# Two narrow columns as the held operand of a norm sum, and weight slices used for both halves in turn

## The reference

```python
def rms_norm(x, gain):
    xf = x.astype(jnp.float32)
    xf = xf * lax.rsqrt(jnp.mean(xf * xf, axis=-1, keepdims=True) + RMS_EPS)
    return (xf * gain.astype(jnp.float32)).astype(x.dtype)
...
        h = h + hierarchical_moe(rms_norm(h, norm_ffn_g[layer]), ...)
    return rms_norm(h, norm_final_g)
...
        h = rmsnorm(x, attn_norm[l])
        q, k, v, g, gk_low, s5_u, rg_x, rg_gate = jnp.split(h @ w_in[l], splits, axis=-1)
...
def conv_ffn(h, w_up, conv_w, conv_b, w_down):
    up, gv = jnp.split(h @ w_up, 2, axis=-1)
    up = causal_dwconv(up, conv_w, conv_b)
    return (jax.nn.gelu(up) * gv) @ w_down
```

## Time and profile before

| | |
|---|---|
| median of 3 runs | 2604.46 us (2601.79 to 2614.28) |
| profiled execution | 2602.0 us |
| its span, first to last instruction | 2600.2 us |
| mean granted TensorE clock | 0.959 |
| TensorE busy | 2436.9 us (94%), 10998 matmuls, 10998 weight loads |
| VectorE busy | 1039.6 us (40%) |
| ScalarE busy | 571.8 us (22%) |
| GpSimd busy | 700.2 us (27%) |

### The profile page before, as it was taken

The page is one execution under the profiler, slowest core; times in us unless marked ns, Lnnn a source line. Parts: engine busy times, 40 slices in busy tenths (PEclk is TensorE's granted clock), DMA queues, the critical chain, the costliest instruction groups (busy, mean ns, idle before and its releaser), DMA issues.

```text
span 2600.2 us, 27514 instructions
## 1 busy us (share of the span) xinstructions
PE 2436.9 (94%) x10998; PEld 1768.3 (68%) x10998; DVE 1039.6 (40%) x1771; ACT 571.8 (22%) x760; POOL 700.2 (27%) x456
## 2 busy tenths in 40 slices
PE   5999999999798599999799999899899999999997
PEld 4888799999675244444644337644588888888885
DVE  6894044445443011111476866621422122122124
ACT  3001265666522111110121004100211011011011
POOL 2332434346120200000302862001133332332321
PEclk9999999999899799999599999789899999999998
DMA  3132122223304566821501110001111111111101
GB/s 139 66 118 94 42 68 72 72 83 110 134 33 162 228 270 270 316 96 73 190 31 49 74 49 30 12 17 37 44 49 37 61 49 37 61 49 37 61 25 73
DMA packets 74348, 228.68 MB, mean 88 GB/s; under 512 B 5168, under 2 KB 36912, under 8 KB 69232
## 3 DMA queue, kind: packets, MB, share of 16 engines
q1 hardware_dynamic: 55712, 141.19, 15.6%
q0 software_dynamic: 12896, 61.09, 6.6%
q10 hardware_dynamic: 5616, 24.64, 2.3%
HBM read 173.42 MB, written 53.48 MB: 87 GB/s over the span
## 4 chain that ended last, share of the span: by engine, by line
PE 91%; DVE 4%; issue 2%; DMA 1%; ACT 1%; POOL 0%; SPq 0%; DVEq 0%; POOLq 0%
PE ps L657 13%; PE ps L659 13%; PE ps L658 13%; PE ps L619 11%; PE ps L814 8%; PE ps L741 7%; PE ps L830 4%; PE ps L723 4%; PE ps L732 3%; PE ps L667 2%; PE ps L639 2%; PE ps L900 1%; PE ps L919 1%; PE ps L805 1%; PE ps L851 1%
## 5 line engine op out<-in xcount | busy, mean ns | idle before, releaser
L657 PE MATMUL ps<-work_part 128*128 128x512 f32 x1472 | 574.3, 390 | 8.9 <-POOL work_part L503 7.2
L659 PE MATMUL ps<-work_part 128*128 128x512 f32 x1472 | 573.3, 389 | 0.0
L658 PE MATMUL ps<-work_part 128*128 128x512 f32 x1120 | 436.4, 390 | 0.0
L501 POOL CAST work_part<-ring 128x1024 fp32r<-128x1024 f32 (+2 forms) x108 | 105.9, 981 | 1055.2 <-PE ps L659 642.4
L657 PEld LDWEIGHTS ps<-work_part 128*128 128x128 f32 x1472 | 276.6, 188 | 67.8 <-issue 8.4
L659 PEld LDWEIGHTS ps<-work_part 128*128 128x128 f32 x1472 | 276.7, 188 | 57.5
L619 PE MATMUL ps<-work,ring 128*128 128x512 f32 x640 | 278.2, 595 | 1.4 <-DVE work L1935 1.4
L503 POOL TENSOR_TENSOR work_part<-ring,work_part 128x1024 fp32r<-128x1024 f32 (+2 forms) x108 | 241.9, 2239 | 8.6
L658 PEld LDWEIGHTS ps<-work_part 128*128 128x128 f32 x1120 | 210.6, 188 | 43.8
L619 PEld LDWEIGHTS ps<-work,ring 128*128 128x128 f32 x640 | 122.1, 191 | 154.8 <-issue 152.9
L814 PE MATMUL ps<-work 128*128 x496 | 219.2, 595 | 1.2 <-SPq L454 0.9
(11 more groups left out here) (309 smaller groups left out, 3023.8 us busy)
## 6 DMA issues: line engine op xcount, KB each, us to landing
work<-w_moe SPq DMA_DIRECT2D x16, 3072.0 KB, 11.0
ring<-w_up_units SPq DMA_DIRECT2D x44, 512.0 KB, 3.3
ring<-w_in_units SPq DMA_DIRECT2D x42, 512.0 KB, 3.3
x_slots<-hT SPq DMA_DIRECT2D x31, 512.0 KB, 3.5
work<-x_slots POOLq DMA_DIRECT2D x31, 512.0 KB, 4.6
y_slots<-work ACTq DMA_DIRECT2D x31, 512.0 KB, 2.6
ring<-w_down_units SPq DMA_DIRECT2D x24, 384.0 KB, 3.0
s_turns<-work ACTq DMA_DIRECT2D x8, 1024.0 KB, 4.0
```

What stands on the lines that cost most here:

```text
L501: pool.tensor_copy(WHI[n % 2][:, 0:cols], w).then_inc(whi_ready, 1)
L657: pe.matmul(ps[:, c], whi[:, w], hi[k][:, c], start=(k == 0), stop=False)
L658: pe.matmul(ps[:, c], whi[:, w], lo[k][:, c], start=False, stop=False)
L659: mm = pe.matmul(ps[:, c], wlo[:, w], hi[k][:, c], start=False, stop=(k == len(hi) - 1))
```

## The change

In the norm sums the operands trade places: the two columns `gain_sums[:, :, k]` are the held weights, the squares stream. The result has the tokens along a row, 2 x 128; ScalarE copies it into `TROW` (two partitions of a free work tile). Behind the last sum eight small transposes (use `P_TTURN`, one wait for each copy) turn it back into 128 x 2 for each tile, and VectorE reads these from PSUM. In `parts_tile` the loop over k is outside; each of the three products is made for both halves before the next, so a weight slice is named by consecutive matmuls: four with `whi`, two with `wlo`. The wait for `ready` stays once for each k.

```diff
--- before.py
+++ after.py
@@ -276,6 +276,7 @@
                 P_YSUM[tt] = take(1)
             if tt >= 1:
                 P_TSUM[tt - 1] = take(1)
+        P_TTURN = take(1)
         P_BOTH, P_FIRST = take(1), take(1)
 
         MAIN = [take(1) for _ in range(3)]
@@ -336,6 +337,7 @@
             emptied[use_s[u]], emptied[use_t[u]], emptied[use_o[u]] = (scores_ready, u + 1), (pT_ready, u + 1), (heads_done, u + 1)
         for i in range(NT):
             emptied[use_f[i]] = (f_ready, i + 1)
+        emptied[P_TTURN] = (tvar_ready, 1)
         emptied[P_BOTH], emptied[P_FIRST] = (hn_ready, NT), (hres_ready, NT)
         emptied[P_LOGIT] = (logit_ready, 1)
         emptied[P_ROUTE], emptied[P_RANK] = (gdiff_ready, 1), (rank_read, 1)
@@ -426,6 +428,7 @@
         YG = [Wp[13 + i] for i in range(2 * NT)]
         TSQ = [Wp[2], Wp[3]]
         TDIAG = [Wp[23], Wp[24]]
+        TROW = Wp[4][0:2, :]
         gain_sums = small[:, 0:2, :]
         both_gains = small[:, 2, :]
         tsums = small[:, 4:6, :]
@@ -648,14 +651,16 @@
                 ps, s = slot(n), split_of[u]
                 pe.wait_ge(wlo_ready, s + 1)
                 whi, wlo = WHI[s % 2], WLO[s % 2]
-                for half in range(2):
-                    c = slice(half * HALF, (half + 1) * HALF)
-                    for k in range(len(hi)):
-                        if ready is not None and half == 0:
-                            pe.wait_ge(ready, base + k + 1)
-                        w = slice(k * P, (k + 1) * P)
+                halves = [slice(half * HALF, (half + 1) * HALF) for half in range(2)]
+                for k in range(len(hi)):
+                    if ready is not None:
+                        pe.wait_ge(ready, base + k + 1)
+                    w = slice(k * P, (k + 1) * P)
+                    for c in halves:
                         pe.matmul(ps[:, c], whi[:, w], hi[k][:, c], start=(k == 0), stop=False)
+                    for c in halves:
                         pe.matmul(ps[:, c], whi[:, w], lo[k][:, c], start=False, stop=False)
+                    for c in halves:
                         mm = pe.matmul(ps[:, c], wlo[:, w], hi[k][:, c], start=False, stop=(k == len(hi) - 1))
                 mm.then_inc(mm_done, 1)
 
@@ -848,9 +853,14 @@
                     pe.wait_ge(tsq_ready, t)
                     ps = slot(P_TSUM[t - 1])
                     for k in range(NT):
-                        mm = pe.matmul(ps[:, 0:2], TSQ[(t - 1) % 2][:, k * P:(k + 1) * P], gain_sums[:, :, k],
+                        mm = pe.matmul(ps[0:2, 0:P], gain_sums[:, :, k], TSQ[(t - 1) % 2][:, k * P:(k + 1) * P],
                                        start=(k == 0), stop=(k == NT - 1))
                     mm.then_inc(mm_done, 1)
+            ps = slot(P_TTURN)
+            for t in range(NT):
+                pe.wait_ge(tsum_taken, t + 1)
+                mm = pe.transpose(ps[:, 2 * t:2 * t + 2], TROW[:, t * P:(t + 1) * P], ident[0:2, 0:2])
+            mm.then_inc(mm_done, 1)
             for i, n in enumerate((P_BOTH, P_FIRST)):
                 pe.wait_ge(tdiag_ready, i + 1)
                 ps = slot(n)
@@ -1183,7 +1193,7 @@
                                    ACT.Square).then_inc(tsq_ready, 1)
                 if t >= 1:
                     act.wait_ge(mm_done, done(P_TSUM[t - 1]))
-                    act.activation(tsums[:, :, t - 1], PS[P_TSUM[t - 1] % SLOTS][:, 0:2], ACT.Copy).then_inc(tsum_taken, 1)
+                    act.activation(TROW[:, (t - 1) * P:t * P], PS[P_TSUM[t - 1] % SLOTS][0:2, 0:P], ACT.Copy).then_inc(tsum_taken, 1)
             act.wait_ge(tvar_ready, 1)
             act.activation(troots, tsums, ACT.Sqrt).then_inc(troot_ready, 1)
             act.wait_ge(hn_ready, NT)
@@ -1738,9 +1748,10 @@
                     ysum(t)
                 if t >= 1:
                     ysum_to_h(t - 1)
-            dve.wait_ge(tsum_taken, NT)
-            ts(tsums[:, 0, :], tsums[:, 0, :], 1.0 / D, EPS, ALU.mult, ALU.add)
-            ts(tsums[:, 1, :], tsums[:, 1, :], 1.0 / D, None, ALU.mult)
+            dve.wait_ge(mm_done, done(P_TTURN))
+            both_sums = PS[P_TTURN % SLOTS][:, 0:2 * NT].rearrange("p (t n) -> p t n", n=2)
+            ts(tsums[:, 0, :], both_sums[:, :, 0], 1.0 / D, EPS, ALU.mult, ALU.add)
+            ts(tsums[:, 1, :], both_sums[:, :, 1], 1.0 / D, None, ALU.mult)
             dve.scalar_tensor_tensor(out=tsums[:, 1, :], in0=tsums[:, 0, :], scalar=EPS, in1=tsums[:, 1, :],
                                      op0=ALU.mult, op1=ALU.add).then_inc(tvar_ready, 1)
             dve.wait_ge(troot_ready, 1)
```

## The result

The changed kernel took 2587.76 us, median of 8 runs (2585.02 to 2596.19). Beside it the kernel before took 2612.24 us (8 runs, 2601.79 to 2614.49). The ratio is 0.9929, with a 95% interval of 0.9911 to 0.9947: faster by 0.7%.

The account below looks back on a forecast made before the run. Bound by a chain of waits led by TensorE's split-weight products, and in the norm sums by slow-clocked TensorE. −13.5 + 0.6 + 0 + 0 − 1.9 = −14.8 us, from the 2604.46 us median to 2589.7 us, range 2585 to 2594.

Parts of the forecast that it names:

- The clock of the sums: In the norm sums, TensorE's granted clock was to rise from 0.50 to full at about 1259.5.
- The period: Norm sums, per token tile: VectorE's 3.12 us replaces TensorE's 5.02; last sum ends at 1278.5, −13.5 us.
- The tail: Behind the last norm sum: longer ScalarE copy (+0.1) and one more TensorE step (0.5), together +0.6 us.
- L868: Products spreading the roots after the norm sums: clock down again, so 0, with bounds −2.5 and +1.0 us.
- The split-weight pass: Split-weight units: 4416 matmuls with the same loads, a steady pass staying at 0.2265 us, so 0.
- rival 2: Split-weight units: held weights aren't loaded again, 35 us more gain, 2554.5 us; chance 0.04.
- rival 3: Split-weight units: alternating banks lengthen a pass by 8.5 ns, +37 us, 2627 us in all; chance 0.06.
- The stall: Last "down" group, first tile: TensorE's 1.93 us wait for k-tile 3's low part goes, −1.9 us (bounds 0 and −2.0).
- Rival 1: Norm sums: clock stays at 0.50, TensorE sets the period at 5.15 us a tile, 2604.2 us, no change; chance 0.14.

## Why the prediction was right

It said 2589.7 us and a change of −14.8. Measured were 2587.76 us and, by the ratio, −0.71%, which is 18.5 us. Inside a group of executions the change is −16 to −17 us, and the steps that the change touches add up to −15.7 (below). So the mechanism was right and each step came out within 1 us, while the close agreement of the level was luck.

- *The clock of the sums.* Forecast: up at about 1259.5. It was up by 1258.70. Sums over half the rows kept it at 0.50, and streaming 128 columns past full weights raised it: the step rested on the right cause, the streamed operand and not the narrow load, and L777 (narrow weights at full clock) and the 64-row products (low clock) were the right rows for it.
- *The period.* Forecast: VectorE's 3.12 us. It is 3.11. Last sum's end: forecast 1278.5, measured 1278.7. −13.5 was −13.4. Two small errors meet here. With the clock up earlier, the sum of tile 6 starts at 1274.74 and not 1274.95. But tile 7's addition didn't follow 1.13 us behind tile 6's: it waited 1.01 us for the transposes, so its square came 0.32 us late for TensorE.
- *The tail.* Forecast +0.6. From the sum's end to L868 it took 3.2 us where it had been 2.8, so +0.4.
- *L868.* Forecast 0, with −2.5 as the lower bound. It took 5.2 us (1281.91 to 1287.15) for 6.0 (1294.85 to 1300.89): −0.8. All of the stretch together: −13.8, from 1255.16 and 1287.15 against 1255.10 and 1300.89.
- *The split-weight pass.* Forecast 0: 2649 matmuls in 600 us before and after. Neither the repeated slice (rival 2) nor the alternating bank (rival 3) changes it. The Trainium skill's page "TensorE: Matmul & The Clock Gate" says under "Step-by-step: what each phase is for" that one load can serve many matmuls. In this kernel each matmul still comes with a load, as the loads in pairs show (11006 of each).
- *The stall.* Forecast −1.9; the wait is gone, and the stretch around it is 1.9 us shorter (729.0 and 727.1).
- *Rival 1's price.* It put a tile without the clock at 5.15 us. With half of the rows, at 0.50, tiles are 5.40 us apart, so the change without the clock would have been about 1 us dearer than that sum has it.
- *What it did not see.* The median before was taken as 2604.46 from three runs. Eight gave 2612.24, since the executions fall in two groups 10 us apart. The level came out near because the median before was 8 us too low, by the shares of the groups, and the median after low by about as much, because most of the 8 runs of the changed kernel fell in the faster group. From 2612.24 the same −14.8 would give 2597.4, outside the range that was stated, and the changed kernel run again has a median of 2593.94, at its upper end. The last norm, from its sum on, took 21.6 us (2561.45 to the span's end) against 22.7. That isn't the change's but the clock's, as the three lines above show.

The Trainium skill's page "TensorE: Matmul & The Clock Gate" says under "Part 4: PE-mode transpose" that transposes don't count as activity for the clock. The earlier trace rows and the rises behind eight transposes in the attention don't bear that out. No run here changed the transposes alone. Why one execution has the full clock in the last part of the attention and the next has not stays open: the kernel is the same, and only the instant at which the clock changes, relative to the work, was seen to differ.

## What to carry to other kernels

A stage in which TensorE is busy all the time can still be bound by a low clock, as here with two streamed columns, or with 64 rows: read the granted clock of the stage's window before counting passes. Let the wide operand stream, or make it wide; the result was the same 23.6 us whether two columns or 128 were loaded. If TensorE waits for other engines ahead of clock-starved work, a few products on constants in that wait can be worth more than they cost: with all of them 2565 to 2570 us, against 2585 to 2588 in the faster group of the changed kernel.

## What the hardware showed that was not expected

- Rows count: 64 of 128 rows with the same streamed columns kept the clock at 0.50 for 39 us, where 128 rows brought it up after 3.5 (one execution with 64 rows).
- The clock depends on what ran before. The attention's mix of 64- and 128-row products ran 24 us at 0.50 without raising the clock, and ran for 27 us at 1.00 once six full passes had gone ahead of it.
- One and the same program has two groups of times, 2601 to 2605 and 2611 to 2615 us before, for the most part from one stretch of 45 or 54 us.
